# The hi and lo halves of the in projection's operand, interleaved tile by tile in one buffer

## The reference

```python
for i in range(DEPTH):                                  # 2 layers
    hn = _rms_norm(x, g_pre[i])
    m, S, buf = _mixer(hn, ...)                         # z = hn @ w_in[i], 2048 -> 7168
    h = x + _rms_norm(m, g_post[i])                     # m = concat(ret_out, conv_out) @ w_out[i]
    e = _rms_norm(p[i] @ w_ple[i], g_ple[i])
    x = h + sigmoid(h @ w_ple_gate[i]) * e
```

## Time and profile before

| | |
|---|---|
| median of 3 runs | 1182.34 us (1182.17 to 1184.18) |
| the profiled execution | 1182.32 us, its span 1180.5 us |
| TensorE matmuls | 10026, busy 99% of the span |
| VectorE, ScalarE, GpSimd busy | 78%, 52%, 7% |

### The profile page before, as it was taken

How to read it: one execution, slowest core, us unless ns; L and a number is a source line. 1 busy time by engine, 2 the same in 40 slices (tenths; PEclk the granted TensorE clock), 3 DMA queues, 4 the chain that set the end, 5 groups by cost and what they waited for, 6 DMA issues and landing times.

```text
span 1180.5 us, 25710 instructions
## 1 busy us (share of the span) xinstructions
PE 1171.4 (99%) x10026; PEld 1160.2 (98%) x10026; DVE 923.2 (78%) x1487; ACT 610.7 (52%) x923; POOL 81.2 (7%) x102
## 2 busy tenths in 40 slices
PE   8999999999999999999999999999999999999998
PEld 8999999999999999999999999999999999999998
DVE  6999999999986543688879988999999774446863
ACT  7344655555556445544543435555665564455341
POOL 0000000000000012101120000000000000121000
PEclk9999999999999999999999999999999999999999
DMA  9666755555555654535556676555565556543462
GB/s 311 197 211 216 229 199 185 211 180 198 188 198 177 231 193 143 179 108 179 178 201 226 218 188 213 184 195 185 211 215 181 168 192 233 178 160 126 162 218 87
DMA packets 44331, 225.84 MB, mean 191 GB/s; under 512 B 6496, under 2 KB 13152, under 8 KB 20704
## 3 DMA queue, kind: packets, MB, share of 16 engines
q1 hardware_dynamic: 34832, 202.90, 50.7%
q10 hardware_dynamic: 9424, 21.90, 5.4%
HBM read 210.97 MB, written 13.81 MB: 190 GB/s over the span
## 4 chain that ended last, share of the span: by engine, by line
PE 98%; DMA 1%; DVE 1%; ACT 1%; SPq 0%; issue 0%
PE accum_all L494 30%; PE accum_all L495 29%; PE accum_all L496 29%; PE accum_all L586 1%; PE accum_all L587 1%; PE accum_all L588 1%; PE ps L561 1%; DMA x<-x_t 1%; PE ps L535 1%; PE ps L569 0%; DVE c_buf L1509 0%; PE ps L544 0%; PE accum_all L641 0%; PE accum_all L642 0%; PE accum_all L643 0%; PE ps L553 0%
## 5 line engine op out<-in xcount | busy, mean ns | idle before, releaser
L494 PE MATMUL accum_all<-a_hi,whi 128*128 128x264 f32 x2016 | 576.5, 286 | 0.0
L495 PE MATMUL accum_all<-a_lo,whi 128*128 128x264 f32 x2016 | 571.3, 283 | 0.0
L496 PE MATMUL accum_all<-a_hi,wlo 128*128 128x264 f32 x2016 | 570.9, 283 | 0.0
L1121 DVE TENSOR_TENSOR wlo<-raw,whi 128x2048 fp32r<-128x2048 f32 x182 | 420.9, 2314 | 172.0 <-ACT whi L758 171.8
L758 ACT ACTIVATE whi<-raw 128x2048 fp32r<-128x2048 f32 x182 | 347.8, 1913 | 156.9 <-DMA raw<-w_in 78.5
L494 PEld LDWEIGHTS accum_all<-a_hi,whi 128*128 128x128 f32 x2016 | 379.7, 188 | 4.0 <-issue 3.2
L495 PEld LDWEIGHTS accum_all<-a_lo,whi 128*128 128x128 f32 x2016 | 380.0, 188 | 0.8
L496 PEld LDWEIGHTS accum_all<-a_hi,wlo 128*128 128x128 f32 x2016 | 378.1, 188 | 0.0
L494 PE MATMUL accum_all<-b_hi,whi 128*128 128x264 f32 x672 | 191.0, 284 | 0.0
L495 PE MATMUL accum_all<-b_lo,whi 128*128 128x264 f32 x672 | 190.4, 283 | 0.0
L496 PE MATMUL accum_all<-b_hi,wlo 128*128 128x264 f32 x672 | 190.2, 283 | 0.0
(11 more groups left out here) (219 smaller groups left out, 1247.1 us busy)
## 6 DMA issues: line engine op xcount, KB each, us to landing
raw<-w_in SPq DMA_DIRECT2D x108, 1024.0 KB, 4.9
raw<-w_out SPq DMA_DIRECT2D x32, 1024.0 KB, 4.9
raw<-w_gate SPq DMA_DIRECT2D x32, 1024.0 KB, 4.9
s_new<-s_ret ACTq DMA_DIRECT2D x16, 512.0 KB, 3.6
ss_out<-s_new ACTq DMA_DIRECT2D x16, 512.0 KB, 2.7
raw<-w_pw SPq DMA_DIRECT2D x8, 1024.0 KB, 5.5
x<-x_t SPq DMA_DIRECT2D x4, 528.0 KB, 7.5
raw<-w_in SPq DMA_DIRECT2D x8, 256.0 KB, 8.5
```

The costliest lines, as they stand in the source:

```text
L494: pe.matmul(accum[bank][:, 0:R], w_hi[:, w:w + P], hi, start=k == 0, stop=False)
L495: pe.matmul(accum[bank][:, 0:R], w_hi[:, w:w + P], lo, start=False, stop=False)
L496: mm = pe.matmul(accum[bank][:, 0:R], w_lo[:, w:w + P], hi, start=False, stop=k == k_tiles - 1)
L1121: v.tensor_tensor(wlo[:, slot, :], raw[:, side, :], whi[:, slot, :].bitcast(F32), ALU.subtract).then_inc(s.lo_ready, 1)
```

## The change

One buffer `a` of [P, KT, 2, R] takes the place of the two. Tile k holds its hi half at byte 2112 k and its lo half right behind it at byte 2112 k + 1056. The names `a_hi` and `a_lo` stay as views of it. The two steps that take a register's tile use a new helper `operand` instead of `rows`, since a tile of one half is now two rows apart from the next. The scratch `e_sq` and `e_sum` moves to tiles 10 to 14 of the new buffer. Its size is that of the two buffers before, so everything behind it keeps its address.

```diff
-    a_hi = sb("a_hi", [P, KT, R], F32R)
-    a_lo = sb("a_lo", [P, KT, R], F32R)
+
+    a = sb("a", [P, KT, 2, R], F32R)
+    a_hi, a_lo = a[:, :, 0, :], a[:, :, 1, :]
...
-    e_sq = [sb(f"e_sq{i}", [P, 2, 2, R], at=sb_at[a][0] + (CT + PT) * R * 4) for i, a in enumerate(("a_lo", "a_hi"))]
-    e_sum = sb("e_sum", [P, 2, R], at=sb_at["e_sq0"][1])
-    assert sb_at["e_sum"][1] <= sb_at["a_lo"][1]
+    e_sq = [sb(f"e_sq{i}", [P, 2, 2, R], at=sb_at["a"][0] + (CT + PT + 2 * i) * 2 * R * 4) for i in range(2)]
+    e_sum = sb("e_sum", [P, 2, R], at=sb_at["e_sq1"][1])
+    assert sb_at["e_sum"][1] <= sb_at["a"][1]
...
+    def operand(half, tile):
+
+        return a[:, :, :, :].rearrange("p k h r -> p (k h r)")[:, bass.ds(tile * 2 * R + half * R, R)]
...
-                nc.scalar.activation(rows(a_hi, t), rows(x, t), ACT.Copy,
+                nc.scalar.activation(operand(0, t), rows(x, t), ACT.Copy,
                                      scale=vec(l + 1, t + V_PRE)).then_inc(s.xhi_ready, 1)
...
-            v.scalar_tensor_tensor(rows(a_lo, t), rows(x, t), vec(l, t + V_PRE), rows(a_hi, t).bitcast(F32),
+            v.scalar_tensor_tensor(operand(1, t), rows(x, t), vec(l, t + V_PRE), operand(0, t).bitcast(F32),
                                    ALU.mult, ALU.subtract).then_inc(s.xin_ready, 1)
```

## The result

The changed kernel is slower: median 1188.20 us of 6 runs (1187.02 to 1189.69) against 1183.05 (1182.17 to 1184.18) for the kernel before, a ratio of 1.0042 with a 95% interval of 1.0031 to 1.0052. The profiled execution took 1188.08 us with a span of 1186.2, which is 5.7 us more than before.

What follows compares the result with a forecast made beforehand. TensorE, busy 99% of the span, was taken to set the end by matmul count times step. The profiled 1182.32 us plus 0 for each edit gave 1182.3, range 1180.5 to 1184.2, no change at 0.90.

Steps and rivals of the forecast that it cites:

- I therefore take 0 for the matmuls: TensorE's matmuls in `gemm`: the step from start to start stays as it was, 0 us for the new layout.
- The three stretches that were to stand for three distances: 376 to 396 us (`c`), 540 to 590 (`b`), 440 to 490 (`b` and `a`): 119.0 to 120.5 ns, taken as one number.
- The fourth distance: From L496 to the next L494, 1056 bytes ahead: step 0.12 us like the others, so the new nearness gains or costs nothing.
- The bounds that it set on its 0, -9.7 and +20 us: Matmul step: 1.6 ns less gains 9.7 us; 10 ns more on each of L495's 2016 matmuls costs 20 us.
- the 0.23 us of L552: Cheapest step per column: 0.23 us for 512 columns, by which 264 columns take 118.6 ns, a gain of 9.7 us.
- the read of lo right behind hi gets slower: Rival at L495, 2016 matmuls: up to 10 ns each, 20 us, 1202.5 us; chance 0.05.
- The late producer: Rival at the layer seam: register instructions make TensorE wait, up to 1.6 us, 1183.9; counted with no change but for 0.01.
- The register arithmetic: Tile addresses at L1127 (VectorE) and L1077 (ScalarE): at most 1.6 and 1.2 us more, 0 for the path.
- the two-tile writes and the scratch: L992 and L1560 write two runs, at worst 2.65 us in all, far from their reader; `e_sq`, `e_sum` keep shapes: 0.
- The sign that the prediction named for its own failure: Wrong if the 50 us stretch from 60 us has another matmul count than that of `b`, or TensorE a new wait.
- the mean durations: Sign of no change: L494, L495 and L496 on the new buffer again at 283 to 286 ns.
- The counts that it compared: Matmuls on TensorE in 50 us stretches: 417 on `a`, 416 on `b`, 415 on `b` and `a`; read as one step.

Runs made afterwards that it cites:

- The far buffers: Kernel before with its two separate buffers, `a_lo` begun 32 bytes later, hi and lo 16,928 bytes apart: ratio 1.0029, median 1186.38 us.
- the stored pairs: Kernel before, two buffers, tile k stored at place k // 2 + k % 2 * 8, read in natural order: ratio 1.0051, median 1188.71 us.
- the first experiments: Against the kernel before: lo buffer 32 bytes later 1.0029; one buffer in blocks of eight tiles 1.0000, of two 1.0020; changed kernel with 1088-byte rows 1.0015.
- 0, 8, 1, 9: Kernel before, contraction tiles of products on the in projection's operand taken in the order 0, 8, 1, 9, 2, 10 and so on: ratio 1.0039, 1187.88 us.
- far and near 64: Hi and lo 64 apart modulo 256. Far: kernel before, lo buffer 64 bytes later, 1.0037. Near: one buffer, two-tile blocks, 1.0020; changed kernel, 1088-byte rows, 1.0015.

## Why the prediction was wrong

The step that failed is "I therefore take 0 for the matmuls", and in it the sentence "The beginnings stay multiples of 32 bytes from the same base, and the old layout used all of the same residues". The set of places is the same, but not the sequence in which TensorE visits them. The far buffers show it with 32 bytes: each half on its own visits the same eight places modulo 256 as before, and the time rises by 0.29%.

The three stretches that were to stand for three distances were one case. Hi and lo are 16,896 = 66 x 256 bytes apart in `a` and in `b`; for `c` the distance that follows from the sizes of the buffers is 61,696 = 241 x 256. All three are 0 modulo 256, so the rows could not show what a 32 does. The fourth distance, 1056 bytes from L496 to the next L494, was real and equal to the new hi-to-lo distance, and I read from its 0.12 us that such a jump is free. It is one jump in a sequence; the stored pairs, which take half of these jumps away, show that a jump has no price of its own. The starts of the earlier trace rows also had 10 ns of resolution, and the stretches 0.3 to 0.7 ns, where 0.4 ns were to be told: the change comes to 5.7 us / 6048 = 0.94 ns for each matmul of the main form, and to 1.39 ns in the convolution's tiles.

The rest by its steps. The bounds that it set on its 0, -9.7 and +20 us, held 5.7 us, but the range of 1180.5 to 1184.2 left them out with 0.09 of the chance. The bound of -9.7 rests on a reading that doesn't hold: the 0.23 us of L552 is a piece of the chain, while by the starts the next matmul, L553, begins 0.32 us after L552 (140.87 and 141.19 us); 0.23 us is what passes from L553 to the matmul behind it. The rival "the read of lo right behind hi gets slower" had the right side and a price of the right kind with 0.05. Its mechanism, that lo lies directly behind hi, fell as the cause with the first experiments, and the place that it named, L495 alone, was wrong: in the convolution's tiles the step from L495 to L496 rose by 2.0 ns and that from L496 to the next L494 by 3.4 ns, while that from L494 to L495 fell by 1.2 ns. The late producer did not happen: no new wait, and 2.45 us to spare at the seam. The register arithmetic came to eight instructions more on VectorE, hidden as forecast; the two-tile writes and the scratch cost nothing. The sign that the prediction named for its own failure, another count from 60 us on than that of `b`, is what the profile shows. Another sign misled: the mean durations stayed at 283 to 286 ns (L499 to L501 on `a`: 284 to 285), as they were to with no change, so they don't show the step. The counts that it compared, 417 and 415 to 416, carry the 2.3 matmuls at the edges, so its 120.2 ns should have been 120.8, and so should its 119.0 to 119.8 for `c`, where 192 matmuls in a row have 120.83 ns; that changes nothing in the argument.

The Trainium skill's formula (TensorE: Matmul & The Clock Gate, section Back-to-back issue gap), which that section gives for the isolated gap of a single matmul, makes an estimated 112.5 ns for 264 columns. The traces don't show it for this stream of a weight load and a matmul by turns: the fastest stretch has 707 matmuls in 85 us, 85 / 704.7 = 120.6 ns. That the step depends on where operands lie at all, which the prediction set beside the formula as a possible reason, is now shown; that the whole excess over the formula stems from it is not.

What stays open is the rule. These runs show that the step depends on the sequence of places modulo 256 that operands and weights are read from, and that no sequence tried made the kernel quicker than equal places for hi and lo with successive tiles 32 bytes on. They do not show why 0, 8, 1, 9 is slow, why far and near 64 differ, why two layers with the same places can differ by 0.55 ns, or what in the memory makes it. That other engines' traffic makes it is unlikely but was not tested by itself: the step of the kernel before is 120.83 ns in the convolution's tiles, where VectorE is busy for 78.67 of 85 us, and in the gate product, where it is busy for 44.07 of 55. The slowing also differs between stages with the same operand: 1.15% in the convolution's tiles of the changed kernel, and 0.67% over 150 matmuls in a row in the gate columns (121.46 to 122.27 ns).

## What to carry to other kernels

Where TensorE sets the end, moving a buffer is not free even if no instruction changes: compare the places of the operands of successive matmuls, and of their weights, modulo 256 bytes with those of the kernel that you start from, and keep their sequence and their distances. Where that can't be done, measure it: no rule from these runs gives the price. A row that is to stand for "another distance" must differ in the thing that the change alters; several rows that agree can be one case seen several times. Price a change in the step by the number of matmuls first: at 6048 of them, 0.4 ns (2.4 us in all) is the line between nothing and something. One step in a timeline of hundredths of a microsecond can't show it; a count over a long stretch nearly can (0.14% for one matmul in 85 us), and two starts hundreds of matmuls apart can.

## What the runs showed of the hardware that was not expected

Thirty-two bytes between the beginnings of two buffers are worth 0.29% (lo half of the operand) and 0.62% (lo half of the weights) of a kernel in which TensorE is busy for 99% of the span, at the same granted clock; `wlo` moved brought no new wait, the lo half moved one of 1.2 us. The same 32 bytes on both halves of the operand together are worth nothing that can be told (1.0004). Under an even mean of 120.83 ns, single steps differ with the place of the operand, from 116 to 129 ns, and repeat within 1 ns every 256 bytes.
